# Biases split over 128 partitions and a router that reads rows ahead of their norm, in a one-core decoder layer

## The chip, the cores and the metric

One core of a Trainium2 chip runs one launch of the kernel. The metric is the device time of a launch in microseconds, the median over runs.

## The reference

One decoder layer over 512 prompt rows and 8 sample rows of width 1024, all in float32. What matters here is what stands behind the mixers:

```python
y_conv, conv_state = conv_mix(c_in, conv_prefix, conv_w, conv_b, conv_ln_g, conv_ln_b)   # causal depthwise, 31 taps
mix = jnp.concatenate([y_pool, y_attn, y_conv], axis=-1) @ w_o
x = layer_norm(DEEPNORM_ALPHA * x + mix, ln1_g, ln1_b)
x = layer_norm(DEEPNORM_ALPHA * x + moe_ffn(x, router_w, router_b, e_w_in, e_b_in, e_w_out, e_b_out), ln2_g, ln2_b)

def layer_norm(x, g, b):
    mu = xf.mean(-1); var = square(xf - mu).mean(-1)
    return (xf - mu) * rsqrt(var + 1e-5) * g + b

def moe_ffn(h, router_w, router_b, ...):     # 32 experts, top 4 of 32
    logits = einsum('md,de->me', xt, router_w) + router_b
    top_v, top_i = top_k(logits, 4);  gates = softmax(top_v)
    # every row through its four experts: x @ e_w_in[e] + e_b_in[e], clamped SwiGLU, @ e_w_out[e] + e_b_out[e]
```

## The kernel before, in words

`first_block` does everything up to the routing of the rows, `moe_block` the experts and the second norm. Each is a block of five instruction streams (SP, POOL, ACT, PE, DVE) that are written out by hand and meet at semaphores; the second block starts when every stream of the first is done. Rows are held in tiles of 128: prompt tiles 0 to 3, and NT = 4 for the eight sample rows. Tiles are worked in the order `TILES = (3, 2, 1, 0)`.

*Opening.* PE projects x with w_in in steps of 32 passes (`project`, L867), into two PSUM banks in turn, so a step waits until its bank was read. DVE multiplies each channel tile with its gate (`glu`, L1189) and runs 31 taps on it (`conv_taps`, L1196 and L1199), three tiles in a row; the sums over channels (`channel_sums`, L896) need all of them. Then pooling, the convolution's norm, and the sample's scores follow.

*Biases.* The experts' biases are added by bf16 matmuls against three bf16 parts of each float32 bias, one part on each of three groups of 32 partitions (one expert on each), the last 32 partitions zero. POOL builds these (`keep_high`, `take_off`, L630 and L635 for `brow`; `keep_high_out`, `take_off_out`, L661 and L664 for `drow`): it loads the biases three times (L619, L621), and rounds and subtracts group by group. `brow` keeps the input biases by column quarters.

*Loop.* Twelve attention steps n (pairs of heads of a tile) run as a software pipeline over n = 0 to 13. Tables say at which n other pieces go in between: `PART_AT` and `REST_AT` the output projection in two parts (L1004 with five row groups of w_o, L1013 with three), `TURN_AT` the transposes of the rows behind the norm (L1098), `LOGITS_AT` the router (L1038 for its bias, L1041), `RANK_AT` each row's rank within its expert (L1113, L1115). On DVE a step has the max of the scores (`masked_max`, L1440), the scaling of the probabilities (`row_norms`, L1448 and L1449), and where due the sum (`rest_sum`, L1373), the moments (`moments1`, L1333) and the norm's two passes over 1024 columns (`normal1`, L1343 and L1346), then the choice of experts (`choose_experts`, L1385 to L1394) and the places in the lists (`place_in_lists`, L1408 to L1418). ACT does the exponentials, square roots (L762) and copies out of PSUM (L802 for turned rows) and stores the rows (L767, L768). PSUM results of the small steps alternate between two halves of a bank (`SLOTS`); a step waits for its half to be freed.

*Tail.* Behind the loop come the second part of the output projection of tile 0, the ranks of tile 1, the turned rows, logits and ranks of tile 0, and `job_table`, which sets the order of the experts' work. POOL writes list entries with indirect DMAs (L652); the lists are loaded again, and the second block starts. There, ring units of 1 MB stream the experts' weights (L277), eight units up and four down for each expert (L1812, L1826).

The norm ahead of the router, before:

```python
            def normal1(i):
                ch.do(V.scalar_tensor_tensor(xr, xr, mv[0:m, 0:1], l1g[0:m], ALU.subtract, ALU.mult))
                d.wait_ge(rstd_ready, NTH[i])
                ch.do(V.reciprocal(mv[0:m, 2:3], mv[0:m, 3:4]))
                V.scalar_tensor_tensor(xr, xr, mv[0:m, 2:3], l1b[0:m], ALU.mult, ALU.add).then_inc(x1_ready, 1)
            def turn_rows1(i):
                pe.wait_ge(x1_ready, NTH[i])
```

## Time and profile before

| | |
|---|---|
| median of 3 runs | 1374.19 us (1374.04 to 1374.82) |
| profiled execution, its own time | 1375.13 us |
| its span, first to last instruction | 1373.2 us |
| mean granted TensorE clock | 0.945 of full speed |
| busy: PE, DVE, ACT, POOL | 86%, 39%, 20%, 21% of the span |
| moved | 463.14 MB, mean 337 GB/s |
| convolution taps on DVE | to 116.6 us |
| first PE work of the experts | 322.2 us |

Times in a trace are microseconds from its first instruction. A row of a timeline gives the start, the time from the first to the last of the merged instructions, the engine (a q behind it means that it is the issue of a DMA), the line, the operation, what it writes and reads, the shape and how many; in brackets the idle time of the engine before it and what ended that. Float32 matmuls are recorded as two passes each. PEclk is the clock granted to TensorE as a share of full speed.

### The profile page before, as it was taken

Reading aid. Unit: us, or ns where it says so; the run is one execution under the profiler, and the core shown is the slowest. Engines: PE = TensorE matmul, PEld = TensorE weight load, DVE = VectorE, ACT = ScalarE, POOL = GpSimd, SP = SyncE. Lnnn points to the kernel's source line nnn. Section 1 sums busy time; section 2 is a strip of 40 time slices with the busy share of each in tenths; the row PEclk is TensorE's granted clock in tenths of the full one; section 3 lists DMA queues with packets and bytes.
Section 4 is the critical chain, followed back from the end, with each engine's and each line's share of the span. In section 5 each row is a group of like instructions: output and inputs, shape, how many; then the busy total and the mean of one; then the engine's idle time right before and its main releaser. Section 6 shows DMA issues by size and latency. Waiting matters only on the chain.

```text
span 1373.2 us, 34108 instructions
## 1 busy us (share of the span) xinstructions
PE 1185.9 (86%) x12516; PEld 532.6 (39%) x12517; DVE 533.3 (39%) x866; ACT 272.9 (20%) x533; POOL 281.9 (21%) x242
## 2 busy tenths in 40 slices
PE   8688999855899999999989999998998989987860
PEld 7577555431333343343233333342333332532220
DVE  3997846653422231324222222222314220432226
ACT  0001333311102221132121212130121211131123
POOL 5900000222121221112211141023121212130113
PEclk9889999957999999999999999999999999998975
DMA  9700680355999999999999999999999999999953
GB/s 335 219 3 0 240 283 33 123 216 204 417 413 411 412 411 413 415 404 406 415 418 410 415 401 413 410 416 402 415 408 414 410 419 393 392 404 419 410 221 126
DMA packets 78828, 463.14 MB, mean 337 GB/s; under 512 B 11908, under 2 KB 19689, under 8 KB 28493
## 3 DMA queue, kind: packets, MB, share of 16 engines
q1 hardware_dynamic: 67931, 438.16, 78.5%
q0 software_dynamic: 8800, 18.26, 5.2%
q10 hardware_dynamic: 2066, 6.32, 1.3%
q8 instruction: 18, 0.29, 0.1%
q14 instruction: 13, 0.11, 0.0%
HBM read 448.29 MB, written 19.48 MB: 341 GB/s over the span
## 4 chain that ended last, share of the span: by engine, by line
PE 54%; DMA 17%; issue 3%; DVE 2%; ACT 0%; SPq 0%; ACTq 0%; DVEq 0%; POOLq 0%; POOL 0%
PE pu L1812 34%; PE rest L1826 18%; DMA ring<-in_e_in 10%; DMA ring<-in_e_out 7%; PE pu L1806 1%; PE rest L1837 1%; DVE fin L2028 0%; DVE bn L2010 0%; DVE xgT L1949 0%; DVE mv L2021 0%; DMA acc_rows<-y,row 0%; DMA fin<-acc_rows 0%; PE rest L1831 0%; ACT y L1892 0%; DMA xq<-x_rows,idx 0%
## 5 line engine op out<-in xcount | busy, mean ns | idle before, releaser
L1812 PE MATMUL pu<-ring,xgT 128*32 128x512 f32 x5248 | 589.6, 601 | 35.3 <-DMA ring<-in_e_in 34.5
L1812 PEld LDWEIGHTS pu<-ring,xgT 128*32 128x32 f32 x5248 | 168.0, 111 | 439.8 <-issue 432.8
L1826 PE MATMUL rest<-ring,hid 128*32 128x256 f32 x5248 | 299.0, 385 | 16.9 <-DMA ring<-in_e_out 11.7
L1979 DVE TENSOR_SCALAR gg<-pu 128x1280 f32<-128x1280 f32 x32 | 47.7, 1492 | 603.6 <-PE pu L1812 603.6
L1735 POOL DMA_INDIRECT acc_rows<-y,row x82 | 110.3, 1346 | 778.4 <-ACT y L1892 737.6
L1826 PEld LDWEIGHTS rest<-ring,hid 128*32 128x32 f32 x5248 | 168.6, 111 | 137.5 <-issue 35.1
L1892 ACT ACTIVATE y<-rest,gate 32x256 f32 x328 | 153.1, 467 | 287.1 <-issue 275.2
L1872 ACT ACTIVATE ss<-gg 128x1280 f32<-128x1280 f32 x32 | 40.7, 1272 | 544.8 <-DVE gg L1979 544.8
L867 PE MATMUL pair<-xt,ring 128*128 128x260 f32 x448 | 104.2, 396 | 20.4 <-DVE conv L1189 14.9
L867 PEld LDWEIGHTS pair<-xt,ring 128*128 128x128 f32 x448 | 88.3, 198 | 35.2 <-DVE conv L1189 15.7
L1725 POOL DMA_INDIRECT xq<-x_rows,idx x82 | 88.3, 1076 | 58.7 <-issue 46.8
L1199 DVE SCALAR_TENSOR_TENSOR conv<-conv,chan_sb 128x512 f32<-128x512 f32 x90 | 86.3, 959 | 3.1
L1806 PE MATMUL pu<-brow,chosen 128*32 128x512 bf16 x328 | 25.1, 403 | 42.6 <-issue 23.5
L1949 DVE STREAM_TRANSPOSE xgT<-xq 128x1280 f32<-128x1280 f32 x33 | 49.6, 1504 | 0.2 <-DMA xq<-x_rows,idx 0.2
L1991 DVE TENSOR_TENSOR uu<-uu,ss 128x1280 f32<-128x1280 f32 x32 | 47.7, 1492 | 1.1
L1996 DVE STREAM_TRANSPOSE hid<-uu 128x1280 f32<-128x1280 f32 x32 | 48.1, 1504 | 0.0
L652 POOL DMA_INDIRECT list_rows<-pairs,spots x20 | 19.9, 994 | 136.7 <-DVE spots L1418 132.1
L1994 DVE CAST chosen_down<-cst 128x32 bf16 x32 | 5.8, 181 | 108.2 <-PE rest L1826 105.1
L1989 DVE SCALAR_TENSOR_TENSOR uu<-uu,gg 128x1280 f32<-128x1280 f32 x32 | 47.5, 1483 | 0.0
L1981 DVE TENSOR_SCALAR uu<-pu 128x1280 f32<-128x1280 f32 x32 | 47.4, 1480 | 0.0
L1004 PE MATMUL pair<-ring,mix 128*128 128x512 f32 x80 | 36.3, 601 | 0.0
L1806 PEld LDWEIGHTS pu<-brow,chosen 128*32 128x32 bf16 x328 | 6.5, 97 | 61.5 <-issue 59.3
(263 smaller groups left out, 589.7 us busy)
## 6 DMA issues: line engine op xcount, KB each, us to landing
ring<-in_e_in SPq DMA_DIRECT2D x256, 1024.0 KB, 23.1
ring<-in_e_out SPq DMA_DIRECT2D x128, 1024.0 KB, 24.5
ring<-in_w_in SPq DMA_DIRECT2D x3, 1536.0 KB, 30.0
ring<-in_w_in SPq DMA_DIRECT2D x5, 512.0 KB, 9.2
ring<-in_w_o SPq DMA_DIRECT2D x1, 2048.0 KB, 11.9
conv<-in_x_prompt SPq DMA_DIRECT2D x1, 2048.0 KB, 13.8
x_rows<-conv ACTq DMA_DIRECT2D x4, 512.0 KB
acc_rows<-conv ACTq DMA_DIRECT2D x4, 512.0 KB
```

Source lines behind the costliest of these rows:

```text
L867: mm = nc.tensor.matmul(b[:, h, 0:HALF], wtile[:, tiles_of(lo, lo + P).start, k], xt[:, k, h * HALF:(h + 1) * HALF], start=k == 0, stop=k ...
L1199: ch.mark(V.scalar_tensor_tensor(cy[:, i, 0:SEQ], u[:, i, t:t + SEQ], taps[:, i, t:t + 1], cy[:, i, 0:SEQ], ALU.mult, ALU.add))
L1725: nc.gpsimd.indirect_dma_start(out=xq[:, u % 2, j], out_offset=None, in_=x1_quarters, in_offset=bass.IndirectOffsetOnAxis(ap=idx4[:, u % A ...
L1735: nc.gpsimd.indirect_dma_start(out=acc_dram, out_offset=bass.IndirectOffsetOnAxis(ap=row4[0:GS, u % AHEAD, j:j + 1], axis=0), in_=y[at, u ...
L1812: mm = nc.tensor.matmul(pu[quarter(c), j], xgT[:, j, k], w[:, :, c * QC:(c + 1) * QC], start=False, stop=k == KT - 1, skip_group_check=True)
L1826: mm = nc.tensor.matmul(py[quarter(c), j], hid[:, j, 2 * q + f], w[:, f, c * QC:(c + 1) * QC], start=False, stop=q == FT // 2 - 1 and f == ...
L1892: ins = nc.scalar.activation(y[to, bass.ds(u % 2, 1), j // NQ, c * QC:(c + 1) * QC].rearrange("p o n -> p (o n)"), py[of, j], ACT.Copy, sc ...
L1949: V.transpose(xgT[:, :, :, :].rearrange("p j k s -> p (j k s)"), xq[:, half].rearrange("p j n -> p (j n)")).then_inc(turned, 1)
L1979: V.tensor_scalar(gg[:, :, :], pu[:, :, 0], SW_LIMIT, None, ALU.min).then_inc(g_ready, 1)
L1989: at.do(V.scalar_tensor_tensor(uu[:, :, :], uu[:, :, :], 1.0, gg[:, :, :], ALU.add, ALU.mult))
L1991: V.tensor_tensor(uu[:, :, :], uu[:, :, :], ss[:, :, :], ALU.mult).then_inc(h_ready, 1)
L1996: V.transpose(hid[:, :, :, :].rearrange("p j f s -> p (j f s)"), uu[:, :, :].rearrange("p j n -> p (j n)")).then_inc(hid_ready, 1)
```

## The change

The biases are loaded once: the 32 experts' rows by column quarters on 128 partitions, 768 columns each (two times 256 of the input bias, 256 of the output bias). POOL rounds and subtracts all three parts on all partitions at once, and 24 DMAs on SP's queue, behind the loads of the cached keys and ahead of the prompt's bias table, put the parts in their places in `brow` and `drow`. ACT's first copy of values now waits for these to land; DVE's write of the convolution's result into the mixer's columns waits for the split, as before.

The router's weights are multiplied by the first norm's scale; a new step `fold` on PE at n = 1 sums them, and the weights times the norm's shift, over the model's width, by matmuls against a matrix of ones. PE turns and multiplies raw rows, as soon as the residual sum is there, and DVE applies the mean and the deviation to the 32 logits of each row. The norm of the rows themselves moves behind that, and the stores with it. The deviation's square root, the sums and the passes get places of their own in the tables, and the ranks of tile 1 go between the halves of the last output projection.

```diff
@@ tables @@
 REST_AT = {3: 5, 2: 8, 1: 11}
+FOLD_AT = 1
+SUM_AT = {3: 5, 2: 8, 1: 12}
 TURN_AT = {3: 6, 2: 9, 1: 12}
+ROOT_AT = {3: 5, 2: 8, 1: 13}
+NORM_AT = {3: 7, 2: 10}
...
@@ SP, behind the loads of cache_k @@
+            sp.wait_ge(split_ready, 1)
+            for part in range(3):
+                to = slice(part * NE, (part + 1) * NE)
+                for c in range(NQ):
+                    of = slice(c * NE, (c + 1) * NE)
+                    sp.dma_start(brow[to, c].rearrange("p a n -> p (a n)"), parts[of, part, 0:2 * QC]
+                                 ).then_inc(bias_rows, 16)
+                    sp.dma_start(drow[to, c * QC:(c + 1) * QC], parts[of, part, 2 * QC:]).then_inc(bias_rows, 16)
...
@@ POOL @@
-            gp.wait_ge(ld["xt2"], 16)
+            for c in range(NQ):
+                gp.dma_start(btok[c * NE:(c + 1) * NE, 0:2 * QC].rearrange("p (a n) -> p a n", a=2),
+                             o["e_brow"].rearrange("e (a c n) -> e c a n", a=2, c=NQ)[:, c]).then_inc(ld["brow"], 16)
+            for c in range(NQ):
+                gp.dma_start(btok[c * NE:(c + 1) * NE, 2 * QC:3 * QC], o["e_bout"][0][:, c * QC:(c + 1) * QC]
+                             ).then_inc(ld["bout"], 16)
...
             for part in range(3):
-                gp.dma_start(btok[part * NE:(part + 1) * NE], o["e_brow"]).then_inc(ld["brow"], 16)
...
+                sp_ch.do(nc.gpsimd.tensor_copy(parts[:, part], btok[:, :]))
+                if part < 2:
+                    sp_ch.do(nc.gpsimd.tensor_tensor(btok[:, :], btok[:, :], parts[:, part], ALU.subtract))
+            gp.sem_inc(split_ready, 1)
...
@@ ACT @@
-            a.wait_ge(brow_ready, 1)
+            a.wait_ge(bias_rows, 2 + 16 * 6 * NQ)
...
             ln1_root(0, NTH[0])
             keep_x1T(0)
+            x1_store(1, NTH[1])
+            top_exps(0, NTH[0])
             x1_store(0, NTH[0])
-            top_exps(0, NTH[0])
...
@@ PE @@
+            def fold_router():
+                b = begin("fold")
+                pe.wait_ge(fold_ready, 2)
+                pe.wait_ge(ld["rb"], 16)
+                for k in range(KT):
+                    nc.tensor.matmul(b[:, 0:NE], C("ones"), rw[:, k], start=k == 0, stop=k == KT - 1)
+                nc.tensor.matmul(b[:, NE:2 * NE], C("ones", 1), rb[:, :], start=True, stop=False)
+                for k in range(KT):
+                    mm = nc.tensor.matmul(b[:, NE:2 * NE], C("ones"), rw_b[:, k], start=False, stop=k == KT - 1)
...
             def router_logits(dst, xT_of, x_wait):
-                nc.tensor.matmul(dst, C("ones", 1)[:, 0:dst.shape[0]], rb[:, :], start=True, stop=False)
...
             def turn_rows1(i):
-                pe.wait_ge(x1_ready, NTH[i])
                 for q in range(2):
+                    emptied(pe, f"rest{2 * i + q}")
...
-            out_rest(0)
-            rank(1)
+            out_rest(0, lambda: rank(1))
...
@@ DVE @@
+            def keep_fold():
+                stepped(d, "fold")
+                V.tensor_scalar(route_sums[:, 0], bank("fold")[:, 0:NE], -1.0, None, ALU.mult).then_inc(fold_kept, 1)
+                V.tensor_copy(route_sums[:, 1], bank("fold")[:, NE:2 * NE]).then_inc(fold_kept, 1)
...
             def choose_experts(i, nth, logits):
-                V.tensor_copy(lg[0:m], logits).then_inc(small_read, 1)
+                V.scalar_tensor_tensor(lg[0:m], route_sums[0:m, 0], mv5[0:m, i, 0:1], logits, ALU.mult, ALU.add
+                                       ).then_inc(small_read, 1)
                 d.wait_ge(small_read, SMALL.index(f"l{i}") + 1)
+                ch.do(V.scalar_tensor_tensor(lg[0:m], lg[0:m], mv5[0:m, i, 2:3], route_sums[0:m, 1], ALU.mult, ALU.add))
...
@@ DVE, behind the loop @@
+            root1(1)
             route(1)
-            ln1(0)
+            shifted1(1)
             weigh(1, NTH[1])
             place(1)
+            rest_sum(0)
+            moments1(0)
+            scaled1(1)
+            root1(0)
+            shifted1(0)
             route(0)
+            scaled1(0)
             weigh(0, NTH[0])
             place(0)
```

On PE, in loop step 1, ahead of the output projection's part 7 (`pair` is PSUM, `rw` the router's weights, `ring` holds w_o). Before:

```order
L1004 MATMUL pair<-ring,mix 128x512 x5
L1063 MATMUL bS<-qkv 128x512 x2
L1004 MATMUL pair<-ring,mix 128x512 x5
L1073 MATMUL bT<-cst,ring 128x128 x8
L1063 MATMUL bS<-qkv 128x512 x2
```

And now:

```order
L1002 MATMUL pair<-ring,mix 128x512 x5
L1071 MATMUL bS<-qkv 128x512 x2
L1011 MATMUL pair<-rw,cst 128x32 x8
L1012 MATMUL pair<-rb,cst 128x32
L1014 MATMUL pair<-xt,cst 128x32 x8
L1002 MATMUL pair<-ring,mix 128x512 x5
L1081 MATMUL bT<-cst,ring 128x128 x8
L1071 MATMUL bS<-qkv 128x512 x2
```

Three groups of 32 columns, the new step, stand between the scores and the part.

On PE, behind the loop: the last probabilities, logits of tile 1, output projection and turned rows of tile 0 (`bT` is PSUM for transposes, `conv` holds the rows, `memb` who chose which expert). Before:

```order
L1038 MATMUL pair<-rb,cst 128x32
L1041 MATMUL pair<-rw,xt 128x32 x8
L1087 MATMUL pair<-ring,qkv 64x128 x2
L1013 MATMUL pair<-ring,mix 128x512 x6
L1113 MATMUL pair<-memb,tri_bf 128x32
L1115 MATMUL pair<-memb,tri_bf 128x32 x3
L1098 MATMUL bT<-cst,conv 128x128 x8
L1038 MATMUL pair<-rb,cst 128x32
L1041 MATMUL pair<-rw,xt 128x32 x8
```

And now:

```order
L1051 MATMUL pair<-rw,xt 128x32 x8
L1095 MATMUL pair<-ring,qkv 64x128 x2
L1024 MATMUL pair<-ring,mix 128x512 x3
L1121 MATMUL pair<-memb,tri_bf 128x32
L1123 MATMUL pair<-memb,tri_bf 128x32 x3
L1024 MATMUL pair<-ring,mix 128x512 x3
L1106 MATMUL bT<-cst,conv 128x128 x8
L1051 MATMUL pair<-rw,xt 128x32 x8
```

The two rank groups stand between two halves of the projection, and no bias matmul is ahead of the logits.

On DVE, at the routing of tile 0 (`conv` holds the rows, `lg` the logits). Before, from the sum of tile 0 on:

```order
L1373 TENSOR_TENSOR conv<-conv,pair 128x512 x2
L1333 BN_STATS bn<-conv 128x6 x2
L1335 BN_AGGR mv<-bn 128x2
L1336 TENSOR_SCALAR mv<-mv 128x1
L1343 SCALAR_TENSOR_TENSOR conv<-conv,mv,xt 128x1024
L1345 RECIPROCAL mv<-mv 128x1
L1346 SCALAR_TENSOR_TENSOR conv<-conv,mv,xt 128x1024
L1400 RECIPROCAL tf<-tf 128x1
L1401 TENSOR_SCALAR pairs<-tf 128x4
```

And now:

```order
L1409 TENSOR_TENSOR conv<-conv,pair 128x512 x2
L1342 BN_STATS bn<-conv 128x6 x2
L1344 BN_AGGR mv<-bn 128x2
L1345 TENSOR_SCALAR mv<-mv 128x1
L1365 SCALAR_TENSOR_TENSOR conv<-conv,mv,xt 128x1024
L1349 RECIPROCAL mv<-mv 128x1
L1360 SCALAR_TENSOR_TENSOR conv<-conv,mv,xt 128x1024
L1416 SCALAR_TENSOR_TENSOR lg<-route_sums,mv,pair 128x32
L1419 SCALAR_TENSOR_TENSOR lg<-lg,mv,route_sums 128x32
```

The two passes over 1024 columns ahead of the logits are the second of tile 1 and the first of tile 0; the second of tile 0 stands behind the choice.

## Rows read from the trace of the kernel before

**Rows 1.** Chain of waits, by line, whole span (the page's part 4).

```profile
PE pu L1812 34%; PE rest L1826 18%; DMA ring<-in_e_in 10%; DMA ring<-in_e_out 7%; PE pu L1806 1%; PE rest L1837 1%; DVE fin L2028 0%; DVE bn L2010 0%; DVE xgT L1949 0%; DVE mv L2021 0%; DMA acc_rows<-y,row 0%; DMA fin<-acc_rows 0%; PE rest L1831 0%; ACT y L1892 0%; DMA xq<-x_rows,idx 0%
```

**Rows 2.** Busy time by stretches; the first line names the columns.

```profile
core 0: us, PE busy (x) PEld busy (x) DVE busy (x) ACT busy (x) POOL busy (x), PEclk, DMA share, GB/s
43.00:58.00 15.00, 14.29 (x64) 12.08 (x64) 14.57 (x14) 0.71 (x2) 14.63 (x14) 1.00 1.03 252
269.20:286.00 16.80, 16.31 (x52) 9.88 (x52) 5.01 (x23) 3.86 (x9) 3.91 (x4) 0.59 0.59 225
322.20:1346.00 1023.80, 925.01 (x11248) 353.52 (x11248) 292.08 (x352) 195.05 (x361) 195.50 (x161) 0.97 0.99 399
```

**Rows 3.** DVE in order of time, 0 to 172: start, duration, instruction, [idle before <- releaser].

```profile
23.32 19.56 DVE L1199 SCALAR_TENSOR_TENSOR conv<-conv,chan_sb 128x512 f32<-128x512 f32 x15
...
63.08 2.15 DVE L1196 TENSOR_SCALAR conv<-conv,chan_sb 128x512 f32<-128x512 f32 x1
65.27 6.16 DVE L1199 SCALAR_TENSOR_TENSOR conv<-conv,chan_sb 128x512 f32<-128x512 f32 x4
...
71.96 20.44 DVE L1199 SCALAR_TENSOR_TENSOR conv<-conv,chan_sb 128x512 f32<-128x512 f32 x26
```

**Rows 4.** Single convolution taps on DVE, two narrow windows of the timeline.

```profile
27.92 1.53 DVE L1199 SCALAR_TENSOR_TENSOR conv<-conv,chan_sb 128x512 f32<-128x512 f32 x1
...
56.81 0.75 DVE L1199 SCALAR_TENSOR_TENSOR conv<-conv,chan_sb 128x512 f32<-128x512 f32 x1
```

**Rows 5.** POOL in order of time, 0 to 150.

```profile
22.31 3.47 POOL L630 CAST brow<-qkv 96x512 bf16<-96x512 f32 x4 [6.40 <-DMA qkv<-in_e_brow]
25.88 6.15 POOL L635 TENSOR_TENSOR qkv<-qkv,brow 32x512 f32<-32x512 f32 x4
...
56.39 0.95 POOL L665 MEMSET drow<- 128x1024 bf16 x1 [0.16 <-POOL brow L630]
```

**Rows 6.** PE in order of time, 0 to 314.

```profile
5.58 37.36 PE L867 MATMUL pair<-xt,ring 128*128 128x260 f32 x160 [5.58 <-DMA ring<-in_w_in]
43.55 14.29 PE L867 MATMUL pair<-xt,ring 128*128 128x260 f32 x64 [0.60 <-DVE conv L1189]
72.09 10.19 PE L867 MATMUL pair<-xt,ring 128*128 128x260 f32 x32 [14.25 <-DVE conv L1189]
...
119.80 2.87 PE L896 MATMUL pair<-conv,cst 128*128 128x260 f32 x12 [0.84 <-DVE conv L1228]
```

**Rows 7.** SP's queue and ACT in order of time.

```profile
8.89 33.49 SPq L529 DMA_DIRECT2D ring<-in_cache_k  x3
...
147.07 0.49 ACT L697 ACTIVATE qkv<-pair 128x384 f32<-128x384 f32 x1
```

**Rows 8.** Loop, 168 to 265: one DVE and two PE rows of the timeline.

```profile
180.94 0.69 DVE L1440 CUSTOM_DVE_ANT_0 ring<-bS,ring 128x512 f32<-128x512 f32 x1
...
223.01 1.01 PE L1073 MATMUL bT<-cst,ring 128*128 128x128 f32 x6 [2.00 <-DVE ring L1449]
...
255.33 1.97 PE L1041 MATMUL pair<-rw,xt 128*128 128x32 f32 x16
```

**Rows 9.** Tail, 269 to 301: five PE, one ACT and two DVE rows of the timeline.

```profile
269.23 1.97 PE L1098 MATMUL bT<-cst,conv 128*128 128x128 f32 x8 [4.46 <-DVE conv L1346]
...
277.72 7.93 PE L1013 MATMUL pair<-ring,mix 128*128 128x512 f32 x12
...
290.96 1.97 PE L1098 MATMUL bT<-cst,conv 128*128 128x128 f32 x8 [5.02 <-DVE conv L1346]
...
293.42 3.62 PE L1041 MATMUL pair<-rw,xt 128*128 128x32 f32 x16
298.85 0.20 PE L1113 MATMUL pair<-memb,tri_bf 8*128 8x32 bf16 x1 [1.80 <-DVE memb L1394]
...
292.11 0.60 ACT L802 ACTIVATE xt<-bT 128x512 f32<-128x512 f32 x1 [3.68 <-PE bT L1098]
...
288.11 1.27 DVE L1343 SCALAR_TENSOR_TENSOR conv<-conv,mv,xt 128x1024 f32<-128x1024 f32 x1
...
300.85 0.16 DVE L1418 SCALAR_TENSOR_TENSOR spots<-spot,wraps 128x4 int32<-128x4 f32 x1
```

More of the change, by code:

```diff
@@ L383, in first_block @@
         bn = sb("bn", [P, 2, 6])
-        mv = sb("mv", [P, 4])
+        mv5 = sb("mv", [P, NT + 1, 4])
+        route_sums = sb("route_sums", [P, 2, NE])
+        rw_b = late[:, 2 * D:2 * D + KT * NE].rearrange("p (k e) -> p k e", e=NE)
         lg = sb("lg", [P, NE])
@@ L615, in _ @@
             nc.gpsimd.memset(chosen4[:, :, :], 0.0).then_inc(zeroed, 1)
-            gp.wait_ge(ld["xt2"], 16)
-            for part in range(3):
-                gp.dma_start(btok[part * NE:(part + 1) * NE], o["e_brow"]).then_inc(ld["brow"], 16)
-            for part in range(3):
-                gp.dma_start(otok[part * NE:(part + 1) * NE], o["e_bout"][0]).then_inc(ld["bout"], 16)
-            gp.wait_ge(zeroed, 4)
-            sp_ch = Chain(gp, split)
-            sp_ch.do(nc.gpsimd.memset(brow[:, :, :, :], 0.0))
@@ L625, in _ @@
-            gp.wait_ge(ld["brow"], 48)
-            by_quarter = lambda lo, hi: btok[lo:hi].rearrange("p (a c n) -> p c a n", a=2, c=NQ)
-            def keep_high(lo, hi):
-                for c in range(NQ):
-                    sp_ch.mark(nc.gpsimd.tensor_copy(brow[lo:hi, c], by_quarter(lo, hi)[:, c]))
-                sp_ch.wait()
-            def take_off(lo, hi):
-                for c in range(NQ):
-                    sp_ch.mark(nc.gpsimd.tensor_tensor(by_quarter(lo, hi)[:, c], by_quarter(lo, hi)[:, c],
-                                                       brow[lo:hi, c], ALU.subtract))
-                sp_ch.wait()
@@ new lines, in _ @@
+            for c in range(NQ):
+                gp.dma_start(btok[c * NE:(c + 1) * NE, 2 * QC:3 * QC], o["e_bout"][0][:, c * QC:(c + 1) * QC]
+                             ).then_inc(ld["bout"], 16)
+            sp_ch = Chain(gp, split)
+            gp.wait_ge(zeroed, 4)
+            nc.gpsimd.memset(brow[3 * NE:, :, :, :], 0.0).then_inc(bias_rows, 1)
+            gp.wait_ge(bias_rows, 1)
+            nc.gpsimd.memset(drow[3 * NE:, :], 0.0).then_inc(bias_rows, 1)
+            gp.wait_ge(bias_rows, 2)
@@ L761, in ln1_root @@
                 a.wait_ge(var_ready, nth)
-                nc.scalar.activation(mv[0:rows(i), 3:4], mv[0:rows(i), 1:2], ACT.Sqrt).then_inc(rstd_ready, 1)
+                nc.scalar.activation(mv5[0:rows(i), i, 3:4], mv5[0:rows(i), i, 1:2], ACT.Sqrt).then_inc(rstd_ready, 1)
             def x1_store(i, nth):
@@ L819, in _ @@
                     ln1_root(NT, 1)
-                for i in REST_AT:
-                    if n == REST_AT[i]:
+                for i in ROOT_AT:
+                    if n == ROOT_AT[i]:
                         ln1_root(i, NTH[i])
@@ L830, in _ @@
                         keep_x1T(i)
+                for i in NORM_AT:
+                    if n == NORM_AT[i]:
                         x1_store(i, NTH[i])
@@ L1006, in out_part, with out_rest @@
                 mm.then_inc(pe_step, 1)
-            def out_rest(i):
+            def fold_router():
[7 more added lines that the diff above has]
+                    mm = nc.tensor.matmul(b[:, NE:2 * NE], C("ones"), rw_b[:, k], start=False, stop=k == KT - 1)
+                mm.then_inc(pe_step, 1)
+            def out_rest(i, between=None):
                 for h in range(2):
+                    if h and between:
+                        between()
                     b = begin(f"rest{2 * i + h}")
@@ L1036, in router_logits @@
             def router_logits(dst, xT_of, x_wait):
[L1038 removed]
                 for k in range(KT):
                     x_wait(k)
[L1041 removed]
+                    mm = nc.tensor.matmul(dst, xT_of(k), rw[:, k], start=k == 0, stop=k == KT - 1)
                 return mm
@@ L1492, in _ @@
                     place_in_lists(NT, 1, ranks_of(NT))
-                for i in REST_AT:
-                    if n == REST_AT[i]:
-                        ln1(i)
+                for i in SUM_AT:
+                    if n == SUM_AT[i]:
+                        rest_sum(i)
+                        moments1(i)
+                for i in NORM_AT:
+                    if n == NORM_AT[i] - 1:
+                        root1(i)
+                        shifted1(i)
+                        scaled1(i)
                 for i in RANK_AT:
```

94 lines of the change are left out of this document (50 added, 44 removed).

## The prediction

> **What bounds the kernel now.** I read the chain of waits first, then the busy time by stretches, then each engine's instructions in order of time. The chain [rows 1] ends in the expert block: matmuls fed by weight transfers, 34% and 18% on PE, 10% and 7% on the transfers. The stretch from 322.2 to 1346 has a DMA share of 0.99 at 399 GB/s [rows 2]: the reader is to see a stream of weights at its limit, about 1024 us long, that starts when the first expert is worked on. The change touches nothing in it, so a microsecond taken from the first block is one off the end, and one taken from an engine there that nobody waits for is nothing. The question is what sets the 322 us ahead.
>
> **The opening (to 119.8).** DVE runs 93 convolution taps in a row. Taps late in the chain go at 20.44/26 = 0.786 us; the first ones at 19.56/15 = 1.304 us (there are two such blocks of 15), then 6.16/4 = 1.54, with one 2.15 us step [rows 3]. All the slow ones lie beside POOL's splitting of the biases, which runs from 22.31 to about 70 [rows 5]. Single taps tell which of two causes it is: 1.53 us beside a POOL TENSOR_TENSOR at 27.92, 0.75 us at 56.81, when POOL was in a memset and the stretch from 43 to 58 still moved 252 GB/s [rows 2, 4, 5]. So it is POOL's reading work, not the traffic. The slowed DVE then holds PE: the projections run to 43, two more follow to 57.8, and the next waits until 72.09 and goes at 10.19 us where half of 14.29 is usual, since the clock fell in the 14.25 us gap [rows 6]. The first matmuls that need the convolution start at 119.80, 0.84 us after PE was free [rows 6].
>
> **The loop (168 to 264.7)** is PE in a row with few gaps; the longest is 2.00 us at 223.01, where PE waited for probabilities that DVE had queued behind the norm [rows 8]. **The tail (264.7 to 301)** is latency: PE idles 4.46 us ahead of the turned rows of tile 1 and 5.02 us ahead of those of tile 0, both for the norm's last pass on DVE, and works at half clock: transposes 1.97, out projection 7.93, logits 3.62 us, placing done at 301.0 [rows 9].
>
> **The change, part by part.**
>
> (1) *Bias split.* POOL's reading steps go from 28 casts and subtractions of 512 columns and 7 of 1024, on 96 or 32 partitions, to 5 of 768 columns on 128. By the rows of 512 columns (3.47/4 = 0.87 and 6.15/4 = 1.54 us [rows 5]), if time goes with columns: 3 x 1.3 + 2 x 2.3 = 8.5 us for 48. The loads are issued at 1.2 us, no longer after 10.9, so the split should be over about when DVE starts at 22. Take DVE's excess away: 2 x (19.56 - 11.8) + (6.16 - 3.1) + (2.15 - 0.8) = 19.9 us; about 1.1 comes back as a wait for the fourth projection (PE ends the fifth at 42.9, so the fourth at 35.8; sixteen taps end near 35). DVE is ready at 119.8 - 19.9 + 1.1 = 101.0. What is late next is PE: seventh and eighth projections end at 50.1 and 57.3, the ninth 7.15 later at 64.4; from there to 119.8 it took 119.80 - 82.28 - 0.84 = 36.7, so 101.1 [rows 6]. The two meet. **Gain 18.7 us.** Bounds: 4.4 (only the slow steps from 63.08 on, when the first loads are over) and 19.9. I take 18.7, by the single taps.
>
> If the split is late and lies beside taps, 48 us of it cost 19.9, so 8.5 cost 3.5 us. The Trainium skill (SBUF — State Buffer, Who interferes with whom) says that a VectorE instruction with two SBUF inputs contends with a GpSimd instruction that reads SBUF, not with one that only writes, that the lock is exclusive for the whole instruction, and that a DMA never contends with an engine. The tap beside the memset agrees; by the exclusive lock 8.5 us beside taps would cost up to 8.5, and the sum would end near 1354, where the price from the rows gives 1349.
>
> The 384 KB of bias loads now go beside the very first inputs, ahead of the first matmul at 5.58 [rows 6]. Between 0 and 1.6 us (393 KB at the 252 GB/s from 43 to 58 [rows 2]); I take **+0.5**, as only the part that lands ahead of those inputs counts.
>
> SP gets 24 small transfers behind the cache loads, whose issue ends at 42.4 [rows 7], and ahead of the prompt bias, needed at 168. ACT waits for them before row 147.07 [rows 7], now near 129. Hidden by 85 us; if that cover were gone, see the third rival.
>
> (2) *Router folded.* DVE's two products over 256 columns fall in its wait for PE after the first scores: nothing. PE gets 17 matmuls of 32 columns, 34 passes, at 1.97/16 = 0.123 us [rows 8] **+4.2**, in a stretch where PE is never idle. The new step takes a PSUM half that the sample's probabilities need next; DVE frees it only behind the two max passes of step 2 (0.69 each [rows 8]) and two small copies, and PE comes to it right after those scores: **+2.1**. The router bias leaves every logits group: about 0.25 each, **-0.7** for three in the loop.
>
> (3) *Raw rows turned.* In the loop the norm's two passes of 1.27 us [rows 9] move behind the next scores. The 2.00 us stall at 223.01 shrinks to ACT's copies of the turned rows (0.6 each [rows 9]): **-1.6**. The other stalls are under 1 us and I leave them. Loop: 4.2 + 2.1 - 0.7 - 1.6 = **+4.0**, bounds 0 and +6.3.
>
> Tail, in the times of the trace before: PE reaches the turned rows of tile 1 at 268.7 and starts at once, since only the residual sum is needed. Full clock 1.0, ACT's copies to 270.5, the last probabilities 0.8, logits 1.8, values 0.4: 273.5. Half of the out projection 2.7, ranks 0.3 (no longer behind the whole), other half 2.7: 279.3. Sum 0.7, moments 1.7 (5.02 less the sum and two passes [rows 9]): 281.7. The turned rows are long there, but ACT's copies stand behind its square root: 282.0 to 283.2. Logits then end at 284.1 at full clock, 286.1 at half; I take 285.3. Choosing took 1.80 [rows 9], two new small operations instead of one copy make 2.0: 287.3. The remaining norm pass 1.3, gates 0.4, placing 1.6: 290.6 against 301.0. With the loop's +4.0 in it: **-10.4**. Bounds: if the clock is at half throughout, projection +2.5, transposes +1.0, logits +1.8: -5; full clock and no wait for ACT: -12.5.
>
> **Sum:** -18.7 + 0.5 - 10.4 = -28.6 us. The profiled execution (span 1373.2, its time 1375.13, so 1.9 around it) would give 1346.5; it lay 0.9 above the median of the runs. From the median: 1374.2 - 28.6 = **1345.6**.
>
> **The rivals.**
> - *Traffic, not POOL, slows the taps.* Then only the 4.4 us from 63 on go: -4.4 + 0.5 - 10.4 = -14.3, 1360. For it: most slow taps lie in a stretch of heavy loading, 252 GB/s from 43 to 58 [rows 2]. Against: the tap at 56.81. 6%.
> - *The tail stays cold and DVE-bound.* The norm passes stand on DVE ahead of placing and routing, and PE's new gaps keep the clock at half; with the loop's full +6.3 the tail and loop give nothing: 1374.2 - 18.2 = 1356. For it: the half clock after both gaps, 0.59 from 269.2 to 286 [rows 2]. Against: the gap at 264.7 that began it goes. 9%.
> - *Slower: ACT's gate.* Should the 24 transfers be held as the three cache loads were (33.49 us of issue for three [rows 7]), ACT reaches its value copies late and frees no PSUM. The gate bites from (129 - 42.4)/24 = 3.6 us each, and outweighs the tail from (147.1 + 10.4 - 42.4)/24 = 4.8 each; at 5.0 the copies start at 162.4, 15.3 later than before, less 10.4: 1379. Against: the queue is full then because of 3 MB of cache rows, and these are 32 KB or less. 2%. The Trainium skill (DMA: Bandwidth & Descriptors, Anatomy of one DMA) gives each DMA a fixed cost of about 2 us, mostly waiting for the write's receipt; paid in turn that would be 48 us, done at 90, still ahead of the gate. No row before shows such a series.
> - *No change:* the shortened block ends at a wait for the first expert's weights or stored rows. Against: at most 8 MB are left to load behind the loop, 21 us at 399 GB/s [rows 2], so from 279.3 they are in by 300.3, and the experts start at 322.2 - 10.4 = 311.8. 2%: 1374.
>
> **Numbers.** My forecast 81%, the rivals 6, 9, 2 and 2. The range 1340 to 1357 takes in the bounds of tail and loop, a late split, and the cold tail; it leaves out the traffic rival and the last two. Faster by over 0.2% (2.7 us, about what a measurement of this kernel can tell from no change): 0.96; within: 0.02; slower: 0.02.
>
> **What would show it.** Right: taps at 0.75 us from the first on; no PE gap of 14 us; the first convolution sums near 101; a group of 32-column matmuls of about 4 us in step 1 and a PE gap of 2 behind it; out projection of tile 0 in two halves of 2.7 with the ranks between; placing done near 272 (301.0 - 29); the expert block as long as before. Wrong: taps slow beside transfers, a wait on SP's queue at ACT's first value copy, or an expert block that grows by what the start gained.

## The result: 15 us faster, half of what was forecast

The changed kernel takes 1359.2 us (median of four, 1357.6 to 1362.0) where the kernel before, run beside it, takes 1374.5 (1374.0 to 1377.1): a ratio of 0.989, 95% interval 0.987 to 0.991. That is 15.3 us faster; the forecast was 28.6, and 1359.2 lies above its range. The profiled execution has a span of 1360.2 us (time 1361.98, the longest of the four). Of all executions behind this document three (one each of e1_pad_pool, e6_after_again and the kernel before) took 2084 to 6106 us in a slow state; every number here leaves them out.

**The profile after.** First the opening. DVE, then POOL, then PE, each in order of time (start, duration, instruction, idle before):

```profile
24.44 0.70 DVE L1198 TENSOR_TENSOR conv<-pair,conv 128x520 f32<-128x520 f32 x1 [24.33 <-PE pair L865]
...
25.76 11.78 DVE L1208 SCALAR_TENSOR_TENSOR conv<-conv,chan_sb 128x512 f32<-128x512 f32 x15
...
55.12 20.45 DVE L1208 SCALAR_TENSOR_TENSOR conv<-conv,chan_sb 128x512 f32<-128x512 f32 x26
```

```profile
11.60 0.82 POOL L651 CAST qkv<-mix 128x768 bf16<-128x768 f32 x1 [2.87 <-DMA mix<-in_e_bout]
12.51 1.63 POOL L653 TENSOR_TENSOR mix<-mix,qkv 128x768 f32<-128x768 f32 x1
...
16.81 0.82 POOL L651 CAST qkv<-mix 128x768 bf16<-128x768 f32 x1
```

```profile
13.55 52.87 PE L865 MATMUL pair<-xt,ring 128*128 128x260 f32 x240 [1.52 <-DMA xt<-in_xT]
...
67.86 35.23 PE L865 MATMUL pair<-xt,ring 128*128 128x260 f32 x160
102.97 2.87 PE L894 MATMUL pair<-conv,cst 128*128 128x260 f32 x12
```

The first fifteen taps take 11.78 us, not 19.56 [rows 3]; the split is over at 17.6, before DVE begins. PE has no gap of 14 us [rows 6], and the first convolution sums come at 102.97, not 119.80: **16.8 us gained**. What does not fit is the start: DVE begins at 24.44, where it began at 22.00 (its first tap stood at 23.32 [rows 3], now at 25.76). Before:

```profile
22.00 0.70 DVE L1189 TENSOR_TENSOR conv<-pair,conv 128x520 f32<-128x520 f32 x1 [21.89 <-PE pair L867]
```

The fast taps have the traffic beside them: the stretch from 24 to 34 (columns as in [rows 2]) moves 419 GB/s while POOL is idle:

```profile
24.00:34.00 10.00, 10.00 (x47) 8.69 (x46) 9.13 (x13) 0.60 (x1) 0.00 (x0) 1.00 1.02 419
```

SP and ACT (first of the 24 transfers, last of them, then the first value copy):

```profile
39.39 0.97 SPq L547 DMA_DIRECT2D brow<-qkv  x1
...
55.43 0.74 SPq L549 DMA_DIRECT2D drow<-qkv  x1
...
127.59 0.49 ACT L692 ACTIVATE qkv<-pair 128x384 f32<-128x384 f32 x1
```

The transfers are out by 56.2 and ACT passes its gate without a wait. Then the loop and the tail on PE:

```profile
154.93 1.97 PE L1011 MATMUL pair<-rw,cst 128*128 128x32 f32 x16
156.84 0.40 PE L1012 MATMUL pair<-rb,cst 1*128 1x32 f32 x2
157.17 1.97 PE L1014 MATMUL pair<-xt,cst 128*128 128x32 f32 x16
...
168.80 0.32 PE L964 MATMUL pair<-cst,s 48*128 48x48 f32 x2 [1.66 <-DVEq L1381]
...
251.26 1.07 PE L1106 MATMUL bT<-cst,conv 128*128 128x128 f32 x8
...
256.62 5.49 PE L1024 MATMUL pair<-ring,mix 128*128 128x512 f32 x6
...
262.24 2.82 PE L1024 MATMUL pair<-ring,mix 128*128 128x512 f32 x6
...
268.48 3.21 PE L1051 MATMUL pair<-rw,xt 128*128 128x32 f32 x16 [1.98 <-ACT xt L797]
...
298.12 1.05 PE L1858 MATMUL pu<-brow,chosen 128*32 128x512 bf16 x8 [11.57 <-DVE xgT L2001]
```

The gaps of 4.46 and 5.02 us [rows 9] are gone; the first half of tile 0's out projection is at half clock (5.49 against 2.82 for the same matmuls), and so are most of the last logits (3.21, 1.94 at full clock). The first expert starts at 298.12, not 322.2: 24.1 us gained ahead of the experts, and only 13.0 left at the end of the span (1360.2 against 1373.2). **The missing 11.1 us are in the expert block, which the change does not touch.** Three places show them. The instruction queue (part 3 of the page: packets, MB, share), before and after:

```profile
q14 instruction: 13, 0.11, 0.0%
```

```profile
q14 instruction: 41, 0.34, 0.1%
```

POOL, at four turns of its loop over six jobs each, and at the end of it, with SP behind:

```profile
560.73 1.06 POOL L1777 DMA_INDIRECT xq<-x_rows,idx  x1 [8.84 <-issue]
...
744.02 1.06 POOL L1777 DMA_INDIRECT xq<-x_rows,idx  x1 [8.90 <-issue]
...
931.18 1.03 POOL L1777 DMA_INDIRECT xq<-x_rows,idx  x1 [9.71 <-issue]
...
1133.63 1.06 POOL L1777 DMA_INDIRECT xq<-x_rows,idx  x1 [7.52 <-issue]
...
1324.97 1.32 POOL L1787 DMA_INDIRECT acc_rows<-y,row  x1 [5.96 <-ACT y L1944]
```

```profile
1332.59 0.72 SPq L1712 DMA_DIRECT2D fin<-acc_rows  x2
```

Before, the same four gathers followed their scatter by 0.67, 0.82, 1.50 and 0.30 us; now they wait 7.5 to 9.7 for nothing that the profile shows. From the last scatter to the first load of the sums it is 7.62 us; before it was 3.40. The kernel before at its first such turn and at the end:

```profile
575.61 1.06 POOL L1725 DMA_INDIRECT xq<-x_rows,idx  x1 [0.67 <-issue]
...
1342.61 1.31 POOL L1735 DMA_INDIRECT acc_rows<-y,row  x1 [5.63 <-ACT y L1892]
```

```profile
1346.01 2.15 SPq L1660 DMA_DIRECT2D fin<-acc_rows  x5
```

And the stretch of the experts by windows, which answers to the last line of [rows 2]:

```profile
298.10:1333.00 1034.90, 928.55 (x11248) 346.96 (x11248) 292.19 (x352) 194.77 (x361) 195.81 (x162) 0.97 0.98 395
```

The same matmuls on the same stream, 11 us longer. The built programs say what POOL's code has to do with it: POOL has 29 instructions fewer ahead of that loop than before, so the loop itself, 336 instructions long and unchanged, lies 29 places earlier in memory. What follows calls "block" the time from the first expert matmul to the end of the span: 1051.0 us before, 1062.1 now.

### The profile page after: what moved, and what is told of

It is laid out like the page before. It is cut to its first block, busy times and chain, and to the rows that moved or that the text cites. A ratio compares the mean times of both kernels' runs of the same rounds, so it can differ in the third digit from the quotient of the medians.

```text
span 1360.2 us, 34174 instructions
## 1 busy us (share of the span) xinstructions
PE 1184.9 (87%) x12540; PEld 521.4 (38%) x12541; DVE 515.8 (38%) x875; ACT 272.8 (20%) x533; POOL 243.1 (18%) x214
## 4 chain that ended last, share of the span: by engine, by line
PE 53%; DMA 18%; issue 4%; DVE 2%; SPq 1%; ACT 0%; DVEq 0%; ACTq 0%; POOLq 0%; POOL 0%
PE pu L1864 33%; PE rest L1878 17%; DMA ring<-in_e_in 13%; DMA ring<-in_e_out 5%; PE pu L1858 1%; PE rest L1889 1%; SPq L281 1%; DVE fin L2080 0%; DVE bn L2062 0%; DVE xgT L2001 0%; DVE mv L2073 0%; PE rest L1883 0%; ACT y L1944 0%; DMA fin<-acc_rows 0%; DVE idx L1993 0%
## 5 line engine op out<-in xcount | busy, mean ns | idle before, releaser
L1864 PEld LDWEIGHTS pu<-ring,xgT 128*32 128x32 f32 x5248 | 162.2, 111 | 450.2 <-issue 449.6
L1878 PE MATMUL rest<-ring,hid 128*32 128x256 f32 x5248 | 298.5, 385 | 20.0 <-DMA ring<-in_e_out 11.8
L865 PE MATMUL pair<-xt,ring 128*128 128x260 f32 x448 | 101.1, 388 | 7.8 <-DMA ring<-in_w_in 6.2
L1208 DVE SCALAR_TENSOR_TENSOR conv<-conv,chan_sb 128x512 f32<-128x512 f32 x90 | 67.7, 752 | 3.1
L1002 PE MATMUL pair<-ring,mix 128*128 128x512 f32 x80 | 39.7, 647 | 0.0
## 6 DMA issues: line engine op xcount, KB each, us to landing
ring<-in_w_in SPq DMA_DIRECT2D x3, 1536.0 KB, 24.3
ring<-in_w_in SPq DMA_DIRECT2D x5, 512.0 KB, 11.2
```

The source lines that it names most:

```text
L865: mm = nc.tensor.matmul(b[:, h, 0:HALF], wtile[:, tiles_of(lo, lo + P).start, k], xt[:, k, h * HALF:(h + 1) * HALF], start=k == 0, stop=k ...
L1208: ch.mark(V.scalar_tensor_tensor(cy[:, i, 0:SEQ], u[:, i, t:t + SEQ], taps[:, i, t:t + 1], cy[:, i, 0:SEQ], ALU.mult, ALU.add))
L1864: mm = nc.tensor.matmul(pu[quarter(c), j], xgT[:, j, k], w[:, :, c * QC:(c + 1) * QC], start=False, stop=k == KT - 1, skip_group_check=True)
L1878: mm = nc.tensor.matmul(py[quarter(c), j], hid[:, j, 2 * q + f], w[:, f, c * QC:(c + 1) * QC], start=False, stop=q == FT // 2 - 1 and f == ...
```

## The experiments

**Position of code or chance (P against S), and the parts alone.** The first four ran on one chip beside the kernel before (1374.3).

e1_pad_pool:

```
             gp.sem_inc(split_ready, 1)
+            for _ in range(58):
+                gp.wait_ge(zeroed, 4)
```

> The changed kernel with 29 more instructions on POOL (repeated waits on a semaphore that is long set, 58 of them in pairs, behind the split), as many as the change took away from that engine: POOL's code in the expert block stands where it stood in the kernel before. Theory P (position of code): the 28 extra packets of the instruction queue (13 before, 41 after) are POOL reloading its loop at each turn and at the end; they leave, the four POOL gaps of 7.5 to 9.7 us at the loop's turn leave, and the 7.6 us from the last scatter to the first load of the sums go back to 3.4. That alone is 4 us, and up to 4 more if the expert block's slow growth (-23.0 at the third expert, -18.1 at the last) is its work too: 1351 to 1355. Rival S (the stream of weights varies by itself, by 4 us between executions of one kernel): packets and gaps may go, but the time stays within 1.5 us of the changed kernel's 1359.2.

Measured: 1350.0 us, the mean of five executions from 1347.3 to 1355.0, whose median is 1347.5 (ratio 0.983, 0.981 to 0.985). That is 9 us less than the changed kernel, 12 by the medians. The trace has 29 instructions more than the changed kernel's (34203, 34174), so two of the waits make one instruction. The page has

```profile
q14 instruction: 15, 0.11, 0.0%
```

and POOL's end and SP's first load read

```profile
1314.54 1.32 POOL L1789 DMA_INDIRECT acc_rows<-y,row  x1 [5.01 <-ACT y L1946]
```

```profile
1317.90 2.14 SPq L1714 DMA_DIRECT2D fin<-acc_rows  x5
```

3.36 us apart. The gaps at the turns are 0.76, 0.56, 1.51 and 0.30; the first:

```profile
548.04 1.06 POOL L1779 DMA_INDIRECT xq<-x_rows,idx  x1 [0.76 <-issue]
```

From its first expert matmul (293.67) to the end of the span it takes 1052.0 us; before took 1051.0, the changed kernel 1062.1. P holds, and more fell to it than I expected.

e2_late_loads (one `gp.wait_ge(ld["xt2"], 16)` ahead of the bias loads, one wait of the padding less):

> As e1_pad_pool, and POOL waits for the second half of x before it issues the eight bias loads, as the kernel before did. If the 2.4 us by which DVE's first instruction came later (24.44 against 22.00) is the bias loads' traffic ahead of the first inputs, DVE starts near 22.0 again, the split ends near 28 and lies beside six taps: by 1.53 against 0.78 us for each tap under a subtraction, 2 x 1.63 us of it cost 1.5 to 3 us of DVE, of which PE's order may hide some. I expect 0.5 to 2 us less than e1_pad_pool. If the 2.4 us come from elsewhere (instruction loads at the start), the same time as e1_pad_pool or 1 us more.

Measured: 1355.2 us, 5 more than e1_pad_pool (8 by the medians): a miss. DVE did start early, but five steps of the split, 23.6 to 31.3, lay beside taps and both sides got slower:

```profile
23.33 15.63 DVE L1211 SCALAR_TENSOR_TENSOR conv<-conv,chan_sb 128x512 f32<-128x512 f32 x15
```

```profile
24.85 1.96 POOL L654 TENSOR_TENSOR mix<-mix,qkv 128x768 f32<-128x768 f32 x1
```

Fifteen taps lost 3.85 us to 7.5 us of the split (by the rows of before, 19.9 us for 48, it would be 3.1). PE then waited 2.77 us ahead of the convolution sums and did part of them at half clock, and the tail fell to half clock too (first expert at 301.52); whether that follows from the gap or is the spread shown below stays open.

e3_bias_alone and e4_router_alone (one half of the diff each; e3 with e1's padding, e4 has POOL's old code):

> The kernel before with the bias split of the change alone (loads, split, 24 transfers on SP), with the same 29 instructions put back on POOL. By the trace of after the opening gained 16.8 us. If a microsecond taken from the first block is one off the end: 1374.5 - 16.8 = 1357.7. If part of it is lost in the expert block whatever POOL's code does (rival S, or a stream that must end when it ends), 1359 to 1363. If the 24 transfers cost something later, a wait on SP's queue shows.

> The kernel before with the router half of the change alone: folded weights, raw rows turned, the norm applied to the logits, out projection of tile 0 in two halves. POOL's code is that of before, so the instruction queue should carry about 13 packets. By the trace of after, loop and tail gained 7.1 us: 1374.5 - 7.1 = 1367.4. If the gain of the tail needs the warm clock that the opening's gap of 14 us spoils, or falls short because ACT comes late, 1369 to 1372.

Measured: 1355.6 us, -18.7 (0.986, 0.985 to 0.988), and 1365.9 us, -8.4 (0.993, 0.992 to 0.995). Blocks of 1051.3 and 1050.9 us, 13 and 14 packets, behind first blocks that are 16.6 and 6.3 us shorter. So with POOL's loop left where it was, both halves give what they gain: no start was lost in the stream. Their sum, 27.1, is 2.8 more than e1_pad_pool's 24.3 (by its median 26.8); the next group shows that the first block of one kernel varies by more than that.

**The same place by another road, and three refinements** (before: 1372.2 in these rounds).

e5_before_moved (the kernel before, with `for _ in range(454): gp.wait_ge(zeroed, 4)` behind its split):

> The kernel before, computing all that it computed, with 227 more instructions on POOL (454 repeated waits, about 4 us of POOL's time near 125, when it has nothing to do until 290). 227 is 29 short of 256, so that POOL's code in the expert block should lie against the blocks of 8 KB in which instructions are loaded as in the changed kernel (it has 29 fewer than before), if those blocks repeat with 128 or 256 instructions. Theory P: about 28 more packets of the instruction queue, POOL gaps of 8 to 9 us at the loop's turns, 4 us more between the last scatter and the sums, and some 5 more in the stream: 1380 to 1384 against 1374.3. If P is wrong and the 9 us between the changed kernel and e1_pad_pool are something else (the length of POOL's split, chance), 1374 within 1.5 us.

Measured: 1384.3 us, 12 more than before (1.0084, 1.0069 to 1.0099). With 227 instructions more (34335, 34108 before) and without a line of the change, the kernel before has got its symptoms:

```profile
q14 instruction: 42, 0.34, 0.1%
```

```profile
583.91 1.06 POOL L1727 DMA_INDIRECT xq<-x_rows,idx  x1 [8.76 <-issue]
```

and a block of 1062.0 us.

> The changed kernel itself once more, on the chip and in the rounds of the others. Theory P and all others: its first block as long as that of e1_pad_pool except for the clock in the tail (298.1 against 293.7 there, of which 4.5 is half clock in the out projection and the logits), its expert block 8 to 11 us longer than that of before, 1357.5 to 1362. If the first block's 4.5 us are chance of an execution, its runs spread over 4 us as before, and those of e1_pad_pool over as much.

Measured (the changed kernel unedited): 1360.1 us. Its profiled execution started the experts at 293.65, as e1_pad_pool did and 4.5 us earlier than the changed kernel's first profile, and took 1062.3 us from there. First the start, then its last logits, which show part of why it differs:

```profile
293.65 1.04 PE L1858 MATMUL pu<-brow,chosen 128*32 128x512 bf16 x8 [11.58 <-DVE xgT L2001]
```

```profile
265.29 1.94 PE L1051 MATMUL pair<-rw,xt 128*128 128x32 f32 x16 [1.98 <-ACT xt L797]
```

1.94 us at full clock, where 268.48 above has 3.21 for the same matmuls. With first blocks of one length, the changed kernel and e1_pad_pool thus differ by the block alone, 1062.3 against 1052.0 us; between the runs it is 9 to 12. And the first block carries a spread: 4.5 us here, and 6.7 between e1_pad_pool and e12_pool_delay below (300.38), whose first blocks have the same code. It goes with where the granted clock falls (0.90 from 150 to 200 in e12, 1.00 in e1).

e9_loads_second (as e2, waiting for `ld["gate0_second"]`):

> As e1_pad_pool, but POOL issues the eight bias loads behind the arrival of the second half of the first weights (about 9 us) in place of at 1.5. Theory: the 2.4 us that DVE starts late are bias traffic ahead of the first inputs, and the second half of x, which now follows, has 2.6 us of slack (landed near 10.9, used from 13.5). Then DVE starts at 22.0 to 22.6, the split runs from 14 to 21 and lies beside no tap: 1.8 to 2.4 us less than e1_pad_pool (1350.0), 1347.6 to 1348.2. Rival: the split ends later than 22 and slows three or more taps (e2_late_loads lost 5 us in this way, more than its 3.9 us of slow taps, since PE then had a gap and fell to half clock): 1350 to 1354.

Measured: 1345.4 us (0.981, 0.979 to 0.982), 2.1 below e1_pad_pool by the medians, on another chip. DVE starts at 22.47, the split runs from 18.93 to 25.1, later than expected, and costs DVE's first scaling step 0.61 us and its first fifteen taps 0.44. PE's convolution sums:

```profile
101.11 2.87 PE L897 MATMUL pair<-conv,cst 128*128 128x260 f32 x12
```

1.9 us ahead of e1_pad_pool's 102.99 (102.97 and 103.07 in the changed kernel's profiles). So the early loads cost 1.9 us of PE's time.

e8_tail_order (`keep_x1T(0)` ahead of `ln1_root(0)` on ACT):

> As e1_pad_pool, with ACT's two copies of tile 0's turned rows ahead of its square root for the same tile (two lines exchanged). In the tail PE waits 1.97 us for these copies ahead of the last logits. Theory: without the root in front the copies are done about 1.3 us sooner, the logits follow, and the root (0.2 us) is still there before DVE needs it: 1.0 to 1.4 us less than e1_pad_pool from the tail on. Rival: DVE's own chain (moments, root, the first norm pass) is what the routing waits for, the PE wait is covered: the PE gap shrinks and moves to the next wait, 0 to 0.3 us.

Measured: 1348.6 us, on another chip than e1_pad_pool and with the same ratio to the kernel before, 0.983: no gain that can be told. The trace favours the rival: PE's wait is gone ahead of the logits and comes back ahead of the ranks, behind DVE:

```profile
270.90 1.93 PE L1053 MATMUL pair<-rw,xt 128*128 128x32 f32 x16
276.91 0.20 PE L1123 MATMUL pair<-memb,tri_bf 8*128 8x32 bf16 x1 [4.08 <-DVE memb L1429]
```

**What it is about the position, and what it costs.**

e10_pad_128 (`range(256)` in e1's lines):

> The changed kernel with 128 more instructions on POOL (256 repeated waits, in pairs) in place of the 29 of e1_pad_pool. The instruction queue's packets are of 8192 bytes. If a packet holds 128 instructions of 64 bytes and what counts is how POOL's loop (336 instructions in the built program) lies against such packets, 128 more change nothing: 41 packets again, gaps of 8 to 10 us at the turns, 1358 to 1362 as the changed kernel. If any sufficiently later place helps (the loop must only come behind something), about 14 packets and 1347 to 1354.

Measured: 1360.1 us, 42 packets, the first turn's gap 8.76 us again, a block of 1063.2. Later is not better: 128 instructions on, the place is as bad, and e5_before_moved (29 short of 256) fits the same period. If one packet of 8192 bytes holds those 128 (64 bytes each), a loop of 336 touches three or four packets, by where it begins; that it is the fourth which is one too many is worked out, not shown. In the changed kernel's packet records three such packets come at each of the four turns, some 5 us apart (553.05, 558.05 and 562.93 at the first), and twelve more in the stream outside them.

e12_pool_delay (a memset into a tile of its own, behind the sixth job of each turn):

```
                         if i < AHEAD:
                             place(i + 1)
+                        else:
+                            nc.gpsimd.memset(idle[:, :], 0.0).then_inc(idled, 1)
+                            gp.wait_ge(idled, t + 1)
```

> As e1_pad_pool (code in the good place), with one memset of 7800 bf16 columns on POOL, some 7 us by 1.80 us for 2048, into a tile of its own, at each of the four turns of its loop: POOL is late with a gather there as it is in the changed kernel, with no instruction loaded. In the changed kernel the expert block lost some 5 us between 600 and 1250 and 4 to 5 at its end. Theory D: the lost time in the stream is the late gathers' (they then meet the weights at another moment): the block grows by 3 to 6 us here too. Theory F: it is the loading itself (8 KB packets among the stream, late issues elsewhere): the block stays at 1052 us and the run at 1350 within 2. In both the 4 us at the end don't come back, since nothing is loaded there.

Measured: 1353.1 us. The gathers are late:

```profile
553.56 7.04 POOL L1837 MEMSET idle<- 128x7800 bf16 x1
...
563.81 1.07 POOL L1781 DMA_INDIRECT xq<-x_rows,idx  x1 [3.22 <-issue]
```

about as late as in the changed kernel, and the stream doesn't mind: the last down pass begins 1008.8 us after the first expert, before 1009.5, in e1_pad_pool 1010.6, in the changed kernel 1015.6. The block's 1054.9, 2.9 over e1_pad_pool's and more than theory F allowed, comes from behind the stream: a fifth memset that I had not counted stands ahead of the last scatter. Theory D falls. What is left for the 6 us is the loading itself, and 24 packets are in that stretch (500 to 1324) where before had one (520 to 1342). With the 4.2 us at the end that is 10.3 of the 11.1; the other 0.8 stays open.

e13_one_packet, e14_sixteen_rows, e15_two_packets (on e9's base; 31 jobs):

```
+                    a.wait_ge(extra, 16 * u)
+                    a.dma_start(spare[0:1, 0:2048], o["e_in"][0, 0, 0:1, 0:2048]).then_inc(extra, 16)
                     sigmoid(u)
```

e14 moves `[0:16, 0:128]` in place of `[0:1, 0:2048]`; e15 has the DMA twice, into two rows.

> As e9_loads_second (instruction loads as before, block of 1050.9 us), with one more DMA per job on ACT's queue: one row of 8192 bytes into a spare row of SBUF, 31 in all, a thousandth of the stream's bytes. Theory E (one engine): a packet of 8 KB takes 0.31 us of one of the 16 DMA engines, each weight unit of 1 MB is complete when the last of the 16 is, and the instruction loads all go through one engine, so 20 more of them in the block (67 KB... 160 KB in all) cost 20 x 0.31 = 6.2 us where 6.5 were measured. If one-row DMAs go through one engine too, the block grows by up to 31 x 0.31 = 9.6 us (less what falls into the first 290 us of it, where the matmuls are the bound: 22 or 23 of them count, 7). If such DMAs are dealt out over the engines in turn, 0.6 us or less. Rival B (bytes or total packets): 0.25 MB at 400 GB/s, 0.6 us.

> As e13_one_packet, the same 8192 bytes in each DMA but as 16 rows of 512 bytes. Theory E: spread over the 16 engines, the block grows by less than 1 us (16 packets of 512 bytes cost each engine one short packet a job). If a DMA on ACT's queue disturbs ACT (0.45 us of issue, a wait for the one before), it grows as in e13_one_packet, and that run says nothing about engines.

> As e13_one_packet, with two such DMAs of one row per job. Theory E with every one-row DMA on the same engine: twice the growth of e13_one_packet, 14 us. Dealt out in turn, or no effect in e13: 1.2 us or less.

Measured:

| | time, us | DMAs added | block, us | over e9 |
|---|---|---|---|---|
| e9_loads_second | 1345.4 | none | 1050.9 | |
| e13_one_packet | 1357.4 | 31 of 1 x 8192 B | 1062.1 | +11.2 |
| e14_sixteen_rows | 1349.6 | 31 of 16 x 512 B | 1051.3 | +0.4 |
| e15_two_packets | 1371.6 | 62 of 1 x 8192 B | 1071.8 | +20.9 |

The blocks are from one profile each. The medians lie 12.0, 4.2 and 26.2 over e9's: the chip is another (the kernel before: 1373.5 for 1372.2), and the experts began 2.3 to 5.9 us later (295.89 to 299.44, for 293.58).

The same bytes cost 11 us in one row and 0.4 in sixteen, and twice the rows cost twice the time. Issuing on ACT's queue is not the cause, since e14 does it as often. ACT's queue in e9, e13 and e14 (part 3 of the page: packets, MB, share):

```profile
q10 hardware_dynamic: 2066, 6.32, 1.3%
```

```profile
q10 hardware_dynamic: 2128, 6.57, 1.3%
```

```profile
q10 hardware_dynamic: 3058, 6.57, 1.3%
```

A one-row DMA is two packets, one of 8192 bytes and one of 4; one of sixteen rows is 32. By the packet records each of the long ones takes 0.31 to 0.32 us, as the stream's own packets of 8192 bytes do and as the instruction packets among them do. I had written that what falls into the first 290 us is hidden, and that was wrong: e13 has no lag through nine down passes, while matmuls are the bound, and 3.8 us at the tenth, as soon as the stream is. The debt was there all along and only fell due. So I read it that all 31 count, 0.36 us each (0.34 in e15). The changed kernel's 23 extra packets at that price are 8 us, at the 0.31 of the expectation 7; its last down pass came 6.1 late.

No view names the engine of a packet, so that the instruction packets all go through one engine of the 16 stays an inference. That the one-row DMAs all meet the same engine is inferred too, but closely: their costs add up to about one packet's time each, where packets dealt out in turn would have cost 0.6 us in all by the expectation, and the cut row costs almost nothing. The Trainium skill (DMA: Bandwidth & Descriptors, Why a DMA increments its semaphore by 16 and not by 1) says that a transfer issued by SP or ACT is spread over the largest number of engines, up to 16, that divides the slowest dimension of more than one on both sides, and always over the lowest-numbered. By its rule sixteen rows get sixteen engines, and transfers that get one engine all meet the same; that one row of 2048 elements got one, its two packets show.

**The version from it.** e7_fold_kept_early moves `keep_fold()` ahead of `masked_max(n)` in the loop, on e9's base; e11_all_three adds e8's order.

> As e9_loads_second, and DVE copies the folded sums ahead of the two max passes of step 2, not behind them. Theory: PE's wait for that half of PSUM (1.65 us in e1_pad_pool, forecast 2.1) becomes 0.3 or less, the max passes start 0.4 later, which nobody waits for; the loop is PE-bound, so 1.2 to 1.5 us less, 1344.0 from 1345.4. Rival: PE then waits for the softmax of the sample, which is behind ACT's exponentials, or the scores of step 3 wait for the later max passes: under 0.5 us.

> As e7_fold_kept_early, with the order of e8_tail_order as well. e8 moved PE's 1.97 us wait onto DVE's chain (its expectation's rival: PE's gap ahead of the ranks grew from 2.22 to 4.08), so at full clock it should give 0.3 us more, and at half clock in the last logits, where DVE waits 1.98 us for them (e9_loads_second), up to 2 us. Expected 1343.0 to 1344.5, which beats both kernels by 15 and 30 us.

Measured: 1344.0 us (0.978, 0.977 to 0.979) and 1343.9 us (0.979, 0.978 to 0.980), before 1373.5: both beat both kernels, by 15 and 30 us, and e8's order adds nothing that can be told. PE's wait in e7:

```profile
169.96 0.32 PE L967 MATMUL pair<-cst,s 48*128 48x48 f32 x2 [0.29 <-DVEq L1384]
```

0.29 us for 1.66.

## Why the prediction was wrong

**The step that failed** is in its first part: "The change touches nothing in it, so a microsecond taken from the first block is one off the end", and with it "the expert block as long as before". The first block gave 24.1 us in one profile of the changed kernel and 28.6 in another (322.2 to 298.12 and to 293.65). That the second is the forecast to the tenth is luck in part: the opening gave 16.7 for a forecast 18.2, loop and tail 11.8 for 10.4. The expert block took 11 back, because removing 29 POOL instructions moved POOL's loop to a place in memory where it is loaded again and again. No term or rival priced a change of place in code; [rows 1] and [rows 2] could not show it, the 13 packets of the instruction queue in the page's part 3 could have raised the question. The last sign of being wrong, an expert block that grows by what the start gained, is what came, for 11 of 24 us, though without a cause named. With the loop put back the kernel gave -24.3, and 1350.0 lies in the range.

The Trainium skill has the rule: Runtime: NRT & Kernel Launch, Instruction fetch mechanics, says that a taken branch whose target is outside the two pages then held has to wait until the target's page is loaded. e1, e5 and POOL's gaps agree. Its blocks of 256 instructions don't: over such blocks a loop of 336 crosses one more in only 79 of 256 places, so two places 128 apart could not both be bad, and the changed kernel and e10 are.

**Point by point.**
- *DVE's excess, 19.9 us from POOL's reading:* right. Taps at 0.785 us from the first; bias alone -18.7, of which its profile shows 16.6 up to the experts, for a forecast 18.2. The split itself took less than the 8.5 forecast, five steps of 0.82 and 1.63, 5.7 us.
- *The traffic rival:* refuted by the same taps, fast beside 419 GB/s. That its 1360 lies next to the measured 1359.2 is chance.
- *PE at 101.1, gain 18.7:* the order of work was right; 101.11 in e9. In the change 102.97, since
- *early bias loads +0.5, 0 to 1.6:* too small. DVE lost 2.4, PE 1.9, above the upper bound: I priced bytes that share the bandwidth, but PE's next operands stood behind them (waits of 0.56 and 1.52 us ahead of 10.04 and 13.55).
- *The split if late, 8.5 us beside taps costs 3.5:* e2 measured 3.85 for 7.5. The exclusive lock of the Trainium skill (SBUF — State Buffer, Who interferes with whom) would have cost up to 7.5; DVE lost half of that, and POOL lost too (7.5 us for the 5.7 of the same steps alone).
- *24 transfers hidden:* right. 0.63 us apart, against the 3.6 from which the gate would bite; a fixed cost of 2 us each was not paid in turn (the section named there is on transfers that GpSimd issues; these are SP's).
- *Fold +4.2:* 4.05 (154.93 to 158.98). *PE's wait +2.1:* 1.66. The stall of 2.00 us at the turned probabilities [rows 8] became 0.34.
- *Loop and tail -10.4, bounds -5 and -12.5:* from the convolution sums to the first expert matmul 202.4 us became 195.2 and 190.6 in the two profiles, -7.3 and -11.8. The loop cost 3.4 for a forecast 4.0 (102.97 to the turned rows at 251.26, against 119.80 to 264.7), and placing is done at 277.1 and 272.6 for the forecast 272. The clock was the unknown, as said; ACT's copies did stand behind its root (1.98 us), but with them first and the last logits at full clock (e8) nothing was gained.
- *The cold tail, 1356:* its mechanism is in part what the first profile shows, but it would not have given 1359.

## What to carry to other kernels

When a change adds or removes instructions on an engine that loops at run time, its loop moves in memory: compare the instruction queue's packets of both pages and look for gaps put down to "issue" at the loop's turns, before a lost gain is explained by anything else. In a kernel bound by a stream over all DMA engines, no transfer beside it should be one long row: cut in sixteen it cost 0.4 us in 31 here, whole 0.36 us each time. A debt made while another engine is the bound is paid when the stream is.

## Not expected of the hardware

- Some 25 instruction packets, 0.2 MB beside 463, came with a stream-bound block 6 us longer, where POOL's lateness alone (e12) cost the stream nothing; leaving the loop cost POOL another 4.2 (7.62 against 3.40).
- One row of 8192 bytes per job cost 11.2 us in 31 jobs, two 20.9, sixteen rows of 512 bytes 0.4.
- POOL's split steps are slowed by DVE's taps as well as the other way: 1.96 us for 1.63, casts 1.17 to 1.19 for 0.82.
